# Attention values taken four blocks at a time beside the recurrence's outputs, and keys rounded once

## The chip, the cores and the metric

The kernel runs on one core of a Trainium2 chip. The metric is the device time of one execution in microseconds (us). The engines are TensorE (PE in the profile, its weight loads PEld), VectorE (DVE), ScalarE (ACT), GpSimd (POOL) and the DMA queues that SyncE (SP) feeds. Each engine takes its instructions in the order in which the kernel writes them, and waits at semaphores.

## The reference

One layer of a hybrid backbone on 256 context tokens (two tiles of 128) and 1024 latent tokens (eight tiles). After a joint input projection come two kinds of heads, then an output projection and a squared-ReLU MLP. The part in question is between the two projections:

```python
# gated linear attention, 8 heads, both directions, chunk by chunk
b = cumsum(g); A = tril(sum_d q*exp(b) * k*exp(-b))
o = (q*exp(b)) @ S + A @ v
S = exp(b_last)*S + (k*exp(b_last-b)).T @ v
# windowed attention, 8 query heads on 2 key heads, blocks of 128 queries
s = concat(q @ k_window.T (masked), q @ k_cache.T) * 64**-0.5
p = softmax(concat(s, sink))
o = p[:, :span] @ v_window + p[:, span:] @ v_cache
```

## The kernel before, in words

`mixer` (L1491) interleaves both. A **unit** u is one tile of 128 queries with one of the two key heads: 20 units, 16 of latent tiles with six or seven key blocks, then four of context tiles with two. That makes 116 blocks. A **slot** w (0 to 57, with two more to drain) takes two blocks. Every engine has its own loop over the slots, and the order inside a slot is written out by hand:

- PE, L1847 onwards. `scores` (L1796) makes the transposed scores of blocks 2w and 2w+1 in `st`: two full products each, a third for the mask. `values` (L1817) multiplies the probabilities of a block with the value rows: 16 small products on tiles of 128*64, accumulated in `pv`. Between them lie two **places**, `ahead((w, 0))` and `ahead((w, 1))`, with the work for later units: `raw_context` and `raw_local` (L1763, L1770), a pair of products whose row maxima are wanted; `queries` (L1755), four transposes; `turn_peaks` (L1781).
- The recurrence's step x (3 to 19) has its scores in slot 2(x-3) (`pe_scores`, L1258: four transposes of the decayed keys, then 16 products on tiles of 64*128) and its outputs in the slot behind (`pe_outputs`, L1276: 64 products on tiles of 128*64). Up to slot 33 an even slot is thus scores of the recurrence, an odd one its outputs.
- ACT: `weights` (L1895) is the exponential of one block's scores into `pT`, a ring of PRING = 4; `high_queries` (L1883) rounds turned queries; `outputs` (L1901) copies a finished unit's `pv`; `act_turned`, `act_output`, `act_decays` serve the recurrence.
- DVE: `top_context` and `top_local` (L1963, L1971) reduce the pair of products of a place to row maxima, `peaks`, `low_queries` and `spread` (L1992, L1958, L2008) prepare a unit, `finish` (L2015) divides. Behind both places of an even slot comes `dve_scores` (L1378: the causal mask on the recurrence's scores), behind those of an odd one `dve_new` (L1360: the state's update, one instruction for each half of the partitions).
- POOL has the recurrence's state and operands, and from slot 5 on, every third slot or so, the merging of finished outputs (`GlaOutput`, L1020); ACT waits in `GlaOutput.act` (L1067) for what SP loads for it.

The places use two banks, `score[:, 0]` and `score[:, 1]`; a product waits (`wait_room`) until the maxima of the last user of its bank are taken. A bank of `st` waits for the exponential before last. Ahead of slot 0 come six **beats** with steps 0 to 2 of the recurrence and seven groups of keys (`Keys`, L1409), which ACT copies twice: rounded into `kdup`, and rounded into the upper half of `khl`.

The PE order of a slot before:

## Time and profile before

| what | value |
|---|---|
| time, median of 3 runs | 1687.52 us (1684.58 to 1689.86) |
| the profiled execution's own time | 1684.21 us |
| its span | 1682.3 us |
| PE busy | 1603.9 us, 95% |
| PE weight loads busy | 1394.7 us, 83% |
| DVE, ACT, POOL busy | 1020.3, 673.6, 1016.3 us |
| beats | 390 to 415.2 us |
| slots 0 to 57 and the drain | 415.2 to 697.5 us |

A busy share says only that an instruction was under way; PE's matmuls overlap, so their durations don't add up, and the distance from one start to the next is what a group of them costs. Which wait binds is read in the order of time.

### The profile page before, as it was taken

Reading aid. Unit: us, or ns where it says so; the run is one execution under the profiler, and the core shown is the slowest. Engines: PE = TensorE matmul, PEld = TensorE weight load, DVE = VectorE, ACT = ScalarE, POOL = GpSimd, SP = SyncE. Lnnn points to the kernel's source line nnn. Section 1 sums busy time; section 2 is a strip of 40 time slices with the busy share of each in tenths; the row PEclk is TensorE's granted clock in tenths of the full one; section 3 lists DMA queues with packets and bytes.
Section 4 is the critical chain, followed back from the end, with each engine's and each line's share of the span. In section 5 each row is a group of like instructions: output and inputs, shape, how many; then the busy total and the mean of one; then the engine's idle time right before and its main releaser. Section 6 shows DMA issues by size and latency. Waiting matters only on the chain.

```text
span 1682.3 us, 31906 instructions
## 1 busy us (share of the span) xinstructions
PE 1603.9 (95%) x11618; PEld 1394.7 (83%) x11618; DVE 1020.3 (61%) x1584; ACT 673.6 (40%) x1192; POOL 1016.3 (60%) x758
## 2 busy tenths in 40 slices
PE   4999999998999888899999999999999999999997
PEld 1998778996777766788888998989978899998996
DVE  2713565666676669455866566575695545545468
ACT  2514224225444345312354444444535444444441
POOL 1711554654574789002487787777898667667682
PEclk9999999999999999999999999999999999999999
DMA  9254565659555455333661322313235132231322
GB/s 331 92 159 137 196 210 175 224 179 263 160 171 158 158 158 152 108 130 142 200 224 57 100 75 75 100 51 99 88 114 174 51 100 72 78 100 50 99 64 100
DMA packets 211450, 225.93 MB, mean 134 GB/s; under 512 B 52752, under 2 KB 171664, under 8 KB 208144
## 3 DMA queue, kind: packets, MB, share of 16 engines
q1 hardware_dynamic: 209248, 224.46, 41.6%
q8 instruction: 70, 1.15, 0.3%
q10 hardware_dynamic: 2096, 0.02, 0.1%
q14 instruction: 36, 0.29, 0.1%
HBM read 177.22 MB, written 47.24 MB: 133 GB/s over the span
## 4 chain that ended last, share of the span: by engine, by line
PE 43%; POOL 4%; DVE 2%; issue 1%; ACT 0%; DMA 0%; SPq 0%; DVEq 0%; ACTq 0%; POOLq 0%
PE ff_banks L3095 8%; PE ff_banks L3096 8%; PE ff_banks L3097 8%; PE ff_banks L3068 7%; PE ff_banks L3070 7%; PE ff_banks L3069 7%; POOL h_whi L2734 1%; POOL h_xop L2332 1%; POOL h_wlo L2746 1%; POOL h_whi L2741 1%; DVE ff_tmp L2935 1%; DVE ff_acc L2925 0%; DMA ff_hb<-in_w_ff 0%; DVE ff_acc L2919 0%; DVE ff_acc L2892 0%
## 5 line engine op out<-in xcount | busy, mean ns | idle before, releaser
L3068 PE MATMUL ff_banks<-h_xop,h_whi 128*128 128x320 f32 x888 | 275.2, 310 | 5.8 <-DVE wo_raw L2872 3.1
L3070 PE MATMUL ff_banks<-h_xop,h_whi 128*128 128x320 f32 x888 | 274.4, 309 | 0.0
L3069 PE MATMUL ff_banks<-h_xop,h_whi 128*128 128x320 f32 x888 | 274.4, 309 | 0.0
L2892 DVE TENSOR_TENSOR ff_acc<-ff_acc,ff_banks 128x512 f32<-128x512 f32 x294 | 199.0, 681 | 99.2 <-PE ff_banks L3097 99.2
L3095 PE MATMUL ff_banks<-h_wlo 128*128 128x512 f32 x600 | 234.3, 390 | 1.6 <-DVE ff_acc L2892 0.8
L3097 PE MATMUL ff_banks<-h_wlo 128*128 128x512 f32 x600 | 233.5, 389 | 0.0
L2734 POOL TENSOR_TENSOR h_whi<-mid_raw,h_whi 128x512 fp32r<-128x512 f32 x149 | 207.2, 1406 | 1.4 <-ACT h_whi L2586 1.4
L2746 POOL TENSOR_TENSOR h_wlo<-mid_raw,h_wlo 128x320 fp32r<-128x320 f32 x128 | 116.6, 913 | 129.6 <-ACT mid_raw L2623 129.6
L3068 PEld LDWEIGHTS ff_banks<-h_xop,h_whi 128*128 128x128 f32 x888 | 166.7, 188 | 9.5 <-issue 4.8
L3069 PEld LDWEIGHTS ff_banks<-h_xop,h_whi 128*128 128x128 f32 x888 | 166.7, 188 | 1.1
L3070 PEld LDWEIGHTS ff_banks<-h_xop,h_whi 128*128 128x128 f32 x888 | 166.7, 188 | 0.0
L972 PE MATMUL prj_banks<-prj_whi,h_hi 128*128 128x304 f32 x480 | 147.8, 308 | 3.3 <-DVE h_lo L341 2.2
L2734 POOL TENSOR_TENSOR h_whi<-ff_tmp,h_whi 128x512 fp32r<-128x512 f32 x63 | 105.5, 1674 | 67.7 <-ACT h_whi L2586 67.7
L974 PE MATMUL prj_banks<-prj_whi,h_lo 128*128 128x304 f32 x480 | 145.2, 303 | 0.0
L973 PE MATMUL prj_banks<-prj_wlo,h_hi 128*128 128x304 f32 x480 | 144.7, 301 | 0.0
L3095 PEld LDWEIGHTS ff_banks<-h_wlo 128*128 128x128 f32 x600 | 112.6, 188 | 25.8 <-DVE ff_acc L2892 1.9
L3096 PE MATMUL ff_banks<-h_whi,h_wlo 128*128 128x512 f32 x340 | 132.4, 389 | 0.0
L3097 PEld LDWEIGHTS ff_banks<-h_wlo 128*128 128x128 f32 x600 | 112.6, 188 | 23.6
L2586 ACT ACTIVATE h_whi<-mid_raw 128x512 fp32r<-128x512 f32 x149 | 89.9, 622 | 97.7 <-DVE mid_raw L2848 91.4
L2616 ACT ACTIVATE mid_raw<-wo_raw 128x320 f32<-128x320 f32 x128 | 60.3, 471 | 160.0 <-DVE wo_raw L2870 66.4
L3096 PE MATMUL ff_banks<-h_wlo 128*128 128x512 f32 x300 | 117.0, 390 | 0.0
L825 ACT ACTIVATE prj_stage<-prj_banks 128x304 f32<-128x304 f32 (+2 forms) x47 | 21.0, 446 | 220.7 <-PE prj_banks L974 133.9
(306 smaller groups left out, 3774.2 us busy)
## 6 DMA issues: line engine op xcount, KB each, us to landing
mid_raw<-in_w_ff SPq DMA_DIRECT2D x124, 512.0 KB, 4.3
mid_raw<-in_w_ada SPq DMA_DIRECT2D x18, 1024.0 KB, 7.2
early_room<-qk_by_channel SPq DMA_DIRECT2D x20, 512.0 KB, 4.1
proj<-prj_stage SPq DMA_DIRECT2D x60, 152.0 KB, 1.9
mid_raw<-in_w_in SPq DMA_DIRECT2D x6, 1216.0 KB, 7.2
early_room<-in_w_ada SPq DMA_DIRECT2D x6, 1024.0 KB, 10.9
decays<-early_room SPq DMA_DIRECT2D x8, 640.0 KB, 4.5
early_room<-decays SPq DMA_DIRECT2D x20, 256.0 KB, 2.9
```

The lines of the kernel that those rows point to most:

```text
L972: pe.matmul(out, x_hi, whi[j][:, k, 0:w], start=(k == 0), stop=False)
L973: pe.matmul(out, x_hi, wlo[j][:, k, 0:w], start=False, stop=False)
L974: mm = pe.matmul(out, x_lo, whi[j][:, k, 0:w], start=False, stop=(k == KD - 1))
L2734: pool.tensor_tensor(lo, source(q, i), hi.bitcast(F32), ALU.subtract).then_inc(w1lo_ready, 1)
L2746: pool.tensor_tensor(ulo[j][c][:, t0:t0 + TH], v[i % 2], uhi[j][c][:, t0:t0 + TH].bitcast(F32), ALU.subtract).then_inc(ulo_ready, 1)
L2892: dve.tensor_tensor(acc[:, p, at], acc[:, p, at], down[n % RING], ALU.add).then_inc(added, 1)
L3068: pe.matmul(out, w_hi[:, k], x_hi[:, k], start=(k == 0), stop=False)
L3069: pe.matmul(out, w_hi[:, k], x_lo[:, k], start=False, stop=False)
L3070: mm = pe.matmul(out, w_lo[:, k], x_hi[:, k], start=False, stop=(k == KH - 1))
L3095: pe.matmul(out, x_hi, w_hi[c][:, at], start=(c == 0), stop=False)
L3096: pe.matmul(out, x_hi, w_lo[c][:, at], start=False, stop=False)
L3097: mm = pe.matmul(out, x_lo, w_hi[c][:, at], start=False, stop=(c == 1))
```

## The change

1. PE's order in a slot becomes: place 0, scores of both blocks, the recurrence's four transposes (`pe_turned`, split off `pe_scores`), place 1, the recurrence's 16 score products, values, the recurrence's outputs, values of a second unit.
2. Values are taken in odd slots alone, four blocks at a time (2w-4 to 2w-1), up to slot 51; from slot 52 two in every slot again. PRING goes from 4 to 6.
3. ACT rounds queries of place 0 before the exponentials of its slot, and copies the turned keys of the recurrence before it rounds queries of place 1 and copies a unit's `pv`.
4. The state's update is put into 256 adjoining columns of its bank, so that one DVE instruction over 128 partitions takes it, where there were two over 64.
5. Keys are copied once by ACT, over all partitions of `khl`; DVE then writes the remainder over its lower half. `kdup` is gone.
6. The places are dealt out anew from the changed `done_slot` and `last_scores`: `finish` of a unit moves to the slot behind its last values, always even up to slot 52.

```diff
-    def pe_scores(self, pe, x):
+    def pe_turned(self, pe, x):
         i, d, t = self.place(x)
         pe.wait_ge(self.ke_ready, x + 1)
         if x:
-            pe.wait_ge(self.new_ready, 2 * x)
+            pe.wait_ge(self.new_ready, x)
         for b in range(self.HP):
             tr = pe.transpose(self.ps[:, 2, b * P:(b + 1) * P], self.ke[:, d, b], self.keep["ident"])
         tr.then_inc(self.tr_ready, 1)
+
+    def pe_scores(self, pe, x):
+        i, d, t = self.place(x)
         pe.wait_ge(self.qe_ready, x + 1)
...
-                mm = pe.matmul(self.ps[rows, 2, c:c + DH], self.kt[:, d, c:c + DH], self.v[:, j, c:c + DH], start=True, stop=True)
+                mm = pe.matmul(self.ps[rows, 2, b * DH:(b + 1) * DH], self.kt[:, d, c:c + DH], self.v[:, j, c:c + DH], start=True, stop=True)
...
-        for half in range(2):
-            rows = slice(half * DH, (half + 1) * DH)
-            upd = self.ps[rows, 2].rearrange("p (b c) -> p b c", c=P)[:, :, half * DH:(half + 1) * DH]
-            dve.tensor_tensor(self.new[rows], upd, self.decayed(d, t, rows, 2), ALU.mult).then_inc(self.new_ready, 1)
+        dve.tensor_tensor(self.new[:, :, :], self.update(), self.decayed(d, t, slice(0, P), 2), ALU.mult).then_inc(self.new_ready, 1)
...
     def act(self, act, n):
         act.wait_ge(self.tr_ready, n + 1)
-        act.activation(self.keys_of(self.kdup, slice(0, P), n), self.turned(slice(0, P), n), ACT.Copy).then_inc(self.dup_ready, 1)
-        act.activation(self.keys_of(self.khl, slice(0, DH), n), self.turned(slice(0, DH), n), ACT.Copy).then_inc(self.hl_ready, 1)
+        act.activation(self.keys_of(self.khl, slice(0, P), n), self.turned(slice(0, P), n), ACT.Copy).then_inc(self.hl_ready, 1)
...
-    QRING, PRING = 4, 4
+    QRING, PRING = 4, 6
...
+        SINGLE = begin[LONG] // 2 - 2
+
+        def group(w):
+
+            if not 1 <= w <= SLOTS or (w % 2 == 0 and w < SINGLE):
+                return []
+            return list(range(max(0, 2 * w - 4) if w % 2 and w <= SINGLE else 2 * w - 2, 2 * w))
...
-                while u + 1 >= QRING and at[0] < done_slot[u + 1 - QRING] - 1:
+                while u + 1 >= QRING and at[0] < last_scores[u + 1 - QRING]:
...
+        def parts(w):
+
+            first = [g for g in group(w) if unit_of[g] == unit_of[group(w)[0]]]
+            return first, group(w)[len(first):]
...
+                    ahead((w, 0))
                     if w < SLOTS:
                         scores(2 * w)
                         scores(2 * w + 1)
-                    ahead((w, 0))
-                    late = 1 <= w <= SLOTS and crossing(w)
-                    if 1 <= w <= SLOTS:
-                        values(2 * w - 2)
-                        if not late:
-                            values(2 * w - 1)
-                    if w == 0:
+                    if w in scores_at:
+                        rec.pe_turned(pe, scores_at[w])
+                    ahead((w, 1))
+                    now, late = parts(w)
+                    if w in scores_at:
                         rec.pe_scores(pe, scores_at[w])
-                    ahead((w, 1))
-                    if w and w in scores_at:
-                        rec.pe_scores(pe, scores_at[w])
+                    for g in now:
+                        values(g)
                     if w in outputs_at:
                         rec.pe_outputs(pe, outputs_at[w])
-                    if late:
-                        values(2 * w - 1)
+                    for g in late:
+                        values(g)
...
                 for w in range(SLOTS + 2):
+                    if (w, 0) in query_at:
+                        high_queries(query_at[w, 0])
                     if w < SLOTS:
                         weights(2 * w)
                         weights(2 * w + 1)
-                    if (w, 0) in query_at:
-                        high_queries(query_at[w, 0])
+                    if w in scores_at:
+                        rec.act_turned(act, scores_at[w])
+                    if (w, 1) in query_at:
+                        high_queries(query_at[w, 1])
                     for u in ending(w):
                         outputs(u)
                         sink_term(u)
-                    if (w, 1) in query_at:
-                        high_queries(query_at[w, 1])
-                    if w in scores_at:
-                        rec.act_turned(act, scores_at[w])
```

DVE's and POOL's order inside a slot is as before.

## Rows read from the trace of the kernel before

**Rows 1.** Windows of beats, slots 0-23, 24-33, 34-57 (columns in its header).
```profile
core 0: us, PE busy (x) PEld busy (x) DVE busy (x) ACT busy (x) POOL busy (x), PEclk, DMA share, GB/s
390.00:415.23 25.23, 19.68 (x266) 16.56 (x266) 21.68 (x43) 14.66 (x29) 16.27 (x18) 0.86 0.91 249
415.23:549.43 134.20, 128.88 (x1964) 102.00 (x1960) 91.83 (x194) 59.75 (x118) 79.87 (x84) 1.00 0.52 164
549.43:611.35 61.92, 55.93 (x833) 44.14 (x829) 40.12 (x83) 24.76 (x50) 51.56 (x50) 0.97 0.44 146
611.35:697.50 86.15, 73.62 (x994) 55.34 (x990) 64.23 (x122) 46.33 (x90) 57.44 (x46) 0.98 0.52 160
```

**Rows 2.** Timeline of PE, slots 14 to 16: start, duration (us), engine, line, operation.
```profile
494.65 0.50 PE L1810 MATMUL mix_st<-mix_qdup,mix_khl 128*128 128x512 f32 x1
...
495.76 1.15 PE L1828 MATMUL mix_pv<-mix_vx,mix_pT 128*64 128x65 f32 x32
496.85 0.73 PE L1768 MATMUL mix_score<-mix_khl,mix_qdup 128*128 128x512 f32 x2
497.41 0.60 PE L1264 MATMUL mix_gla<-keep_mats,early_ke 128*128 128x128 f32 x4
497.94 1.16 PE L1272 MATMUL mix_gla<-early_qe,early_ke 64*128 64x128 f32 x16
499.04 0.49 PE L1810 MATMUL mix_st<-mix_qdup,mix_khl 128*128 128x512 f32 x1
...
500.29 0.52 PE L1778 MATMUL mix_score<-mix_khl,mix_qdup 128*128 128x384 f32 x2
...
501.82 1.01 PE L1768 MATMUL mix_score<-mix_khl,mix_qdup 128*128 128x512 f32 x2
502.75 0.69 PE L1285 MATMUL mix_gla<-early_room,early_kt 128*64 128x64 f32 x16
...
505.18 0.49 PE L1810 MATMUL mix_st<-mix_qdup,mix_khl 128*128 128x512 f32 x1
```

**Rows 3.** Timelines of PE's weight loads, 32 and 16 values, and of scores between full tiles.
```profile
500.73 1.01 PEld L1828 LDWEIGHTS mix_pv<-mix_vx,mix_pT 128*64 128x64 f32 x32 [0.25 <-ACT mix_pT L1899]
512.49 0.55 PEld L1828 LDWEIGHTS mix_pv<-mix_vx,mix_pT 128*64 128x64 f32 x16 [0.36 <-ACT mix_pT L1899]
...
418.70 0.39 PE L1810 MATMUL mix_st<-mix_qdup,mix_khl 128*128 128x512 f32 x1
...
419.63 1.04 PE L1768 MATMUL mix_score<-mix_khl,mix_qdup 128*128 128x512 f32 x2
```

**Rows 4.** Timeline of DVE, slot 15.
```profile
499.22 1.23 DVE L1383 TENSOR_TENSOR early_at<-mix_gla,keep_mats 128x1024 f32<-128x1024 f32 x1 [0.48 <-PE mix_gla L1272]
500.87 0.62 DVE L1985 CUSTOM_DVE_ANT_0 mix_junk<-mix_score,mix_maskr,mix_topc 128x384 f32<-128x384 f32 x1 [0.42 <-PE mix_score L1778]
...
502.36 1.29 DVE L1969 TENSOR_REDUCE mix_topc<-mix_score 128x1 f32<-128x512 f32 x2
503.56 0.86 DVE L1367 TENSOR_TENSOR mix_new<-mix_gla,keep_dec 64x256 f32<-64x256 f32 x2
```

**Rows 5.** Timeline of PE, a place behind queries in slot 2; late values in slot 45.
```profile
429.31 0.47 PE L1768 MATMUL mix_score<-mix_khl,mix_qdup 128*128 128x512 f32 x1 [1.00 <-DVE mix_qlow L1960]
...
659.87 0.69 PE L1828 MATMUL mix_pv<-mix_vx,mix_pT 128*64 128x65 f32 x16 [1.17 <-ACT mix_sums L1905]
```

**Rows 6.** Timeline of ACT behind slot 24.
```profile
559.26 0.63 ACT L1071 ACTIVATE mid_raw<-mid_raw 128x512 f32<-128x512 f32 x1 [5.49 <-DMA mid_raw<-proj]
...
560.75 0.60 ACT L1887 ACTIVATE mix_qdup<-mix_score 128x512 fp32r<-128x512 f32 x1
```

**Rows 7.** Waits, 415 to 700: who waited for whom, total us, times, longest.
```profile
ACT mid_raw L1071 <- DMA mid_raw<-proj: 15.6, 4, 5.5
```

**Rows 8.** Timeline of DVE, beats.
```profile
397.72 0.88 DVE L1394 TENSOR_TENSOR mix_state_p<-mix_gla,keep_dec 64x256 f32<-64x256 f32 x2
...
407.17 0.88 DVE L1394 TENSOR_TENSOR mix_state_p<-mix_gla,keep_dec 64x256 f32<-64x256 f32 x2
```

More of the change, by code:

```diff
@@ L1316, in decayed, with update @@
         return self.dec[rows, d, :, t, which:which + 1].broadcast_to([rows.stop - rows.start, self.HP, DH])
+    def update(self):
+        return self.ps[:, 2, 0:self.HP * DH].rearrange("p (b c) -> p b c", c=DH)
     def dve_first(self, dve):
@@ L1334, in wait_state @@
         if x < 2:
-            eng.wait_ge(self.new_ready, 2 * x + 2)
+            eng.wait_ge(self.new_ready, x + 1)
         else:
@@ L1354, in pool_state @@
         pool.tensor_tensor(self.kept[:, :, :], st[:, d], self.decayed(d, t, slice(0, P), 1), ALU.mult).then_inc(self.kept_ready, 1)
-        pool.wait_ge(self.new_ready, 2 * x + 2)
+        pool.wait_ge(self.new_ready, x + 1)
         pool.wait_ge(self.kept_ready, x - 1)
@@ L1390, in dve_state @@
             dve.wait_ge(self.ds_ready, x + 1)
-            for half in range(2):
-                rows = slice(half * DH, (half + 1) * DH)
-                upd = self.ps[rows, 2].rearrange("p (b c) -> p b c", c=P)[:, :, half * DH:(half + 1) * DH]
-                dve.tensor_tensor(st[rows, d], upd, self.decayed(d, t, rows, 2), ALU.mult).then_inc(self.new_ready, 1)
+            dve.tensor_tensor(st[:, d], self.update(), self.decayed(d, t, slice(0, P), 2), ALU.mult).then_inc(self.new_ready, 1)
             return
@@ L1398, in dve_state @@
         dve.wait_ge(self.ds_ready, x + 1)
-        for half in range(2):
-            rows = slice(half * DH, (half + 1) * DH)
-            upd = self.ps[rows, 2].rearrange("p (b c) -> p b c", c=P)[:, :, half * DH:(half + 1) * DH]
-            dve.tensor_tensor(self.new[rows], upd, self.decayed(d, t, rows, 2), ALU.mult).then_inc(self.new_ready, 1)
-        dve.wait_ge(self.new_ready, 2 * x + 2)
+        dve.tensor_tensor(self.new[:, :, :], self.update(), self.decayed(d, t, slice(0, P), 2), ALU.mult).then_inc(self.new_ready, 1)
+        dve.wait_ge(self.new_ready, x + 1)
         dve.wait_ge(self.kept_ready, x - 1)
@@ L1423, in __init__, with work @@
         self.k_in, self.kc_in = s.sem("k_in"), s.sem("kc_in")
-    def work(self, s, keep, kdup, khl, kone, score, st, pv):
-        self.keep, self.kdup, self.khl, self.kone, self.score, self.st, self.pv = keep, kdup, khl, kone, score, st, pv
-        self.tr_ready, self.dup_ready, self.hl_ready, self.low_ready, self.one_ready = (s.sem("keys_" + n) for n in (
-            "tr_ready", "dup_ready", "hl_ready", "low_ready", "one_ready"))
+    def work(self, s, keep, khl, kone, score, st, pv):
+        self.keep, self.khl, self.kone, self.score, self.st, self.pv = keep, khl, kone, score, st, pv
+        self.tr_ready, self.hl_ready, self.low_ready, self.one_ready = (s.sem("keys_" + n) for n in (
+            "tr_ready", "hl_ready", "low_ready", "one_ready"))
     def room(self, n):
@@ L1514, in mixer @@
         rec.rest(s)
-        kdup = s.sb("kdup", [P, KV, NB * P], F32R)
         khl = s.sb("khl", [P, KV, NB * P], F32R)
@@ L1547, in mixer @@
         stored = ahead.mixed
-        keys.work(s, keep, kdup, khl, kone, score, st, pv)
+        keys.work(s, keep, khl, kone, score, st, pv)
         glo = GlaOutput(s, keep, a, scratch, *(arena[:, 2 * m * GW:2 * (m + 1) * GW].rearrange("p (j n) -> p j n", j=2) for m in range(4)),
@@ L1579, in mixer @@
         first_slot = [begin[u] // 2 for u in range(U)]
-        done_slot = [(begin[u] + count[u] - 1) // 2 + 1 for u in range(U)]
+        last_scores = [(begin[u] + count[u] - 1) // 2 for u in range(U)]
+        SINGLE = begin[LONG] // 2 - 2
[3 more added lines that the diff above has]
+            return list(range(max(0, 2 * w - 4) if w % 2 and w <= SINGLE else 2 * w - 2, 2 * w))
+        assert [g for w in range(SLOTS + 1) for g in group(w)] == list(range(total)), (SINGLE, [group(w) for w in range(SLOTS + 1)])
+        value_slot = {g: w for w in range(SLOTS + 1) for g in group(w)}
+        done_slot = [value_slot[begin[u] + count[u] - 1] for u in range(U)]
+        assert len(set(done_slot)) == U
         BEATS = 6
@@ L1836, in _ @@
                         if k % 2 == 0:
+                            rec.pe_turned(pe, k // 2)
                             rec.pe_scores(pe, k // 2)
```

12 lines of the change are left out of this document (5 added, 7 removed).

## The prediction, made before the changed kernel was run

> **What bounds the kernel now.** I read the page first: PE is busy 95% of the span, so whatever the change brings must come out of PE's order of time. The windows [rows 1] then show that the stretch that the change touches, beats and slots, lasts 307.5 us. PE is busy 129 of 134 us in slots 0 to 23, but DVE too is at 92, and in slots 24 to 33 POOL is at 52 of 62. No engine waits for nothing here; three are nearly full.
>
> The timeline of PE [rows 2] and that of DVE beside it [rows 4] show how they interlock. A place's pair of products keeps both banks of `score` until DVE has reduced them: 1.29 us for the cache's scores (at 502.36), 1.4 us for the window's (500.87 to 502.3), and 0.6 us pass from the product's start to the reduction's (500.29 to 500.87). The next place's first product waits for the first maximum, its second for the second. In the odd slot 15 DVE is late, because the mask on the recurrence's scores (1.23 us) comes first in its order: PE's 16 score products end at 499.04, the mask runs 499.22 to 500.45, the first place's maxima run to 502.3, and the second place, issued at 501.82, is held until 502.75. Before the change PE has the 1.09 us of `values` in that gap; what is left open is 0.93 us for a pair that costs 0.56 elsewhere (496.85 to 497.41).
>
> **The change, part by part.** I write R for the moment when the recurrence's score products end.
>
> *Switches between tile shapes.* Values between full tiles last 1.09 us [rows 2]. Their 16 further weight loads take 1.01 - 0.55 = 0.46 us [rows 3], so 32 products are worth 0.92, and 0.17 goes in leaving. The scores in front of them, with a change of shape on either side, last 1.11 us (494.65 to 495.76) [rows 2] against 0.93 between full tiles [rows 3]: 0.18 more. A trip to the small tiles and back costs 0.35 us. Every slot up to 33 makes one for its values; afterwards none does, since those of the odd slots adjoin the outputs. Slots 34 to 51 make nine in place of 18, and the late half of slot 38 had one. That is 33 + 9 + 1 = 43 trips, 15.1 us.
>
> The profile shows the 0.35 us as a late start. The Trainium skill, "TensorEngine Tiling (Array Packing)", section "Key Properties", says that changing the tiling mode drains TensorE; by that rule alone the change would gain all 43 trips, which is the first rival.
>
> *The common pair of slots (14 and 15 and their like).* Even slot, afterwards: scores 1.04 (one change of shape), transposes 0.53, place 0.56, score products 1.10 [rows 2]: 3.2 us; before it was 499.04 - 494.65 = 4.39. Odd slot, afterwards: the place 1 of the even slot is issued 1.66 before R, DVE has reduced it at R + 0.25, the mask ends at R + 1.5, the first place's maxima at R + 2.2 and R + 2.9, so the second place's second product starts at R + 2.95, and values at R + 3.3. PE by itself would be there at R + 2.2. Four blocks take 1.84, the outputs 505.18 - 502.75 = 2.43: R + 7.6. Before it was 6.14 (499.04 to 505.18). The pair takes 10.8 after 10.5. The 0.7 us of two trips is gone, and a wait of 1.1 has come in place of 0.4, because values no longer fill it. The values of an odd slot moved behind the second place; that is the step on which all hangs.
>
> *The other pairs, laid out in the same way.* Their times before are distances between starts of scores in the same timeline, of which [rows 2] show three; [rows 1] have their sum. Slots 8 and 9: 11.0 after 12.8, because before an exponential stood ahead of the rounded queries there. Slots 2 and 3: 12.6 and 12.6; PE had waited 1.00 [rows 5] for ACT's two exponentials, which now stand behind; the first place of slot 3 now pays the mask. Where queries and peaks come in place 1 of an even slot (10, 16, 22), ACT rounds them only after two exponentials and the copy of the turned keys, and DVE has remainder, spread (0.7 each) and mask in a row: maxima start at R + 2.7, values at R + 4.4: 12.4 to 12.6 after 11.5, 11.9 and 11.6. Where they come in place 1 of an odd slot (7, 13, 19), the peaks wait for the first place: values at R + 3.5, 11.2 to 11.35 after 10.2, 11.1 and 10.7. Slots 4 and 5: 11.2 and 11.2. Slots 20 and 21, all four places full: 11.1 after 10.1. Slots 0 and 1: 10.0 and 10.0. Slots 2 to 23 sum to +3.7 us.
>
> *Slots 24 to 33.* At slot 24 ACT waits for a load of the merging until 559.26 [rows 6], 9.8 us after the outputs end. Before, PE went on to slot 26 before it missed the rounded queries. Now they are in place 0 of slot 25, 3.6 us behind the outputs, and values and outputs stand behind the place that needs them: values at 12.7, the pair 17.0 after 11.0. Slots 26 and 27 give 2.2 back (10.7 after 12.9), 28 and 29 2.3 (12.7 after 15.0, which had a wait for POOL), 30 and 31 cost 0.2, 32 and 33 0.3. Sum: 63.9 after 61.9 [rows 1], +2.0. POOL's own work there, 51.6 us, would allow less but not much less than 60.
>
> *Slots 34 to 57.* Ten trips give 3.5 back. Queries rounded ahead of exponentials give about 0.5 in each of 34, 47 and 53, and the load of slot 36 is issued earlier, as no store stands before it: 1.2 over slots 34 to 37. Against it: a unit's last values and the next one's first adjoin in slots 35, 39, 45 and 49, with ACT's copy (0.39 and its way, 0.7 to 1.2) between, as at 659.87 [rows 5]: 3.6 for 1.2. Place 1 of an even slot and place 0 of the next now adjoin with no work between: about 1 us each in 35, 39, 41 and 43. My sum is 86.2 after 86.1 [rows 1]: +0.1.
>
> *Beats.* ACT saves seven copies of some 0.48, which it does at a stretch; the chain there runs over DVE, which saves 0.44 at 397.72 and again at 407.17 [rows 8], and 0.2 by the earlier rounding: slot 0 starts some 1.2 us earlier. The remainder is computed as before. In the slots the same merged update (0.86 for two [rows 4]) lies under the outputs, in which DVE has nothing else to do: nothing. If that cover failed it would be worth 0.44 a pair.
>
> *Sum.* -1.2 + 0 + 3.7 + 2.0 + 0.1 = +4.6 us. The profiled execution took 1684.2 us in all, 3.3 under the median of 1687.5, so it becomes 1688.8, and the median **1692.1 us**. What follows the slots is bound by PE and shifts with them.
>
> **Rivals.** *The trips count in full.* If the second place of an odd slot waits no longer than before, the gain is 15.1 + 1.2 less 2.4 for the late values: -13.9, 1673.6 us; with half of the new waits it would be about 1682. For it: DVE is only 68% busy, so that a reordering may find room. Against it: DVE's order is not changed, and the mask stands ahead of the maxima in every odd slot [rows 4].
>
> *They cancel.* PE's new waits take just what the switches gave, POOL sets the pace in 24 to 33, beats give 1: 1687 us. For it: POOL's 52 of 62 us.
>
> *ACT's waits for loads come out on PE (slower).* Slot 24's 5.5 us wait [rows 6] is one of four, 15.6 us in all [rows 7]. In every odd slot values and outputs now stand behind a place that may need ACT's rounding; before, the values stood ahead of it. If each of the other three costs 3 us as in slot 25, and the recurrence's state, started later, delays POOL by 2, the sum is +4.6 + 9 + 2: 1703 us. It decides when a load lands more than 4 us behind the outputs. For it: the next load is issued while the recurrence's are under way. Against: three of the four lay in slots with a free place.
>
> *The change doesn't do what it says* can be left at the merged update: the same 256 columns in twice the partitions must take 0.42, not 0.86; if not, the beats give nothing.
>
> **How the numbers follow.** Forecast 0.37, give or take 5 us, as each pair is laid out to 0.3 us; trips in full or half 0.26; cancel 0.17; loads 0.20. What a measurement of this kernel can tell from no change is about 0.3%, 5 us: 1682.5 to 1692.6. The forecast lies half inside it. Faster: the first rival and a little: 0.28. Same: cancel and half the forecast: 0.34. Slower: the rest, 0.38. The range of 8 in 10 goes from half way into the first rival to half way to the last: 1677 to 1700 us.
>
> **What would show it.** PE's timeline of slots 14 and 15: the second place of slot 15 must start its second product 2.9 us behind R, with a wait put down to DVE's maximum; values start at R + 3.3 and last 1.84. The waits of PE for DVE's maxima must grow by some 10 us over the slots. Scores between full tiles must last 0.93. Slot 25 must show a stall of 5 us for the rounded queries. If values start at R + 2.3, the chain over DVE was wrong and the first rival holds; if slots 24 to 33 take under 62 us, the step on loads was.

## The result, and the profile after

The changed kernel takes 1712.28 us in the median of four runs (1710.40 to 1719.08), the kernel before in the same comparison 1686.59 (1684.58 to 1689.86). The ratio is 1.0158, with a 95% interval of 1.0125 to 1.0190: slower by 26 us. The forecast had the sign and missed the size: +4.6, and a range that ended at 1700.

The page of the changed kernel, first lines (busy time of each engine, its share of the span, and instructions):

```profile
span 1710.9 us, 31877 instructions
## 1 busy us (share of the span) xinstructions
PE 1612.0 (94%) x11618; PEld 1400.2 (82%) x11618; DVE 1010.1 (59%) x1564; ACT 670.4 (39%) x1185; POOL 1014.2 (59%) x758
```

The span grew by 28.6 us, PE's busy time by only 8: the time is in PE's waits. DVE has 10 us less to do; the merged update accounts for most of that. To see where the time went, I cut both traces at the same places, the first score product of slots 2, 24, 34 and 57. Windows of the kernel before, then of the changed one: slots 2 to 23, then 34 to 56; the changed kernel has slots 24 to 33 between (columns as in [rows 1]).

```profile
425.24:549.43 124.19, 119.34 (x1832) 94.45 (x1828) 83.78 (x173) 55.57 (x110) 73.17 (x74) 1.00 0.51 161
...
611.35:693.21 81.86, 69.33 (x918) 51.78 (x914) 63.47 (x119) 43.41 (x83) 57.44 (x46) 0.98 0.54 165
```

```profile
427.78:557.57 129.79, 117.56 (x1829) 94.14 (x1826) 80.67 (x163) 55.12 (x111) 73.89 (x74) 0.99 0.49 154
...
557.57:625.14 67.57, 56.55 (x834) 45.10 (x832) 38.84 (x78) 24.84 (x51) 51.78 (x50) 0.92 0.41 134
625.14:722.72 97.58, 76.00 (x912) 55.08 (x910) 59.40 (x118) 42.90 (x83) 53.60 (x45) 0.91 0.45 139
```

| stretch | before | after | difference | forecast |
|---|---|---|---|---|
| ahead of the beats | 389.99 | 391.56 | +1.6 | 0 |
| beats, up to slot 0's scores | 25.24 | 26.57 | +1.3 | -1.2 |
| slots 0, 1 | 10.01 | 9.65 | -0.4 | 0 |
| slots 2 to 23 | 124.19 | 129.79 | +5.6 | +3.7 |
| slots 24 to 33 | 61.92 | 67.57 | +5.7 | +2.0 |
| slots 34 to 56 | 81.86 | 97.58 | +15.7 | +0.1 |
| behind that | | | -0.9 | 0 |

The tail, slots 34 to 56, holds more than half, and there the forecast had nothing. In slots 2 to 23 PE is busy 1.8 us less and idle 7.4 more (12.2 for 4.85). In the tail it is idle 9.1 more and busy 6.7 more, at a granted clock of 0.91 instead of 0.98.

PE's timeline of slot 15 in the changed kernel shows the step on which the forecast said all hung (its answer in the kernel before is [rows 2]); the first row is place 0, issued as the recurrence's 16 score products end:

```profile
503.63 0.65 PE L1786 MATMUL mix_score<-mix_khl,mix_qdup 128*128 128x384 f32 x2
504.11 0.40 PE L1818 MATMUL mix_st<-mix_qdup,mix_khl 128*128 128x512 f32 x1
...
505.72 0.47 PE L1776 MATMUL mix_score<-mix_khl,mix_qdup 128*128 128x512 f32 x1 [0.28 <-DVE mix_topl L1992]
506.40 0.50 PE L1776 MATMUL mix_score<-mix_khl,mix_qdup 128*128 128x512 f32 x1 [0.21 <-DVE mix_topl L1992]
506.82 2.09 PE L1836 MATMUL mix_pv<-mix_vx,mix_pT 128*64 128x65 f32 x64
508.74 0.64 PE L1288 MATMUL mix_gla<-early_room,early_kt 128*64 128x64 f32 x16
```

With R = 503.63 the second product starts at R + 2.8, the values at R + 3.2, and 64 of them take 1.92. The forecast had 2.95, 3.3 and 1.84. The marks in brackets add to only 0.5 us, because a wait is shown in full only where nothing of the engine's is still draining; the distances between starts give it: 505.72 to 506.82 is 1.10 for a pair that costs 0.56 elsewhere [rows 2], and it starts some 0.4 us later than behind scores without a wait.

In slots 24 and 25 the stall that the forecast named is there. The products of place 1 in slot 25 wait for rounded queries; the rows are PE's, then ACT's:

```profile
567.72 0.76 PE L1776 MATMUL mix_score<-mix_khl,mix_qdup 128*128 128x512 f32 x1 [5.17 <-DVE mix_qlow L1967]
```

```profile
565.74 0.63 ACT L1071 ACTIVATE mid_raw<-mid_raw 128x512 f32<-128x512 f32 x1 [5.54 <-DMA mid_raw<-proj]
566.28 0.58 ACT L1894 ACTIVATE mix_qdup<-mix_score 128x512 fp32r<-128x512 f32 x1
```

What it did not name is in the tail. Slot 37 first, ACT and then PE. PE's scores of that slot start at 638.39. ACT stands idle until they are through, and only then rounds the queries which place 1 needs (its pair starts at 640.90):

```profile
639.44 0.60 ACT L1894 ACTIVATE mix_qdup<-mix_score 128x512 fp32r<-128x512 f32 x1 [2.40 <-PE mix_st L1821]
```

```profile
638.39 0.48 PE L1818 MATMUL mix_st<-mix_qdup,mix_khl 128*128 128x512 f32 x1
...
640.90 0.47 PE L1776 MATMUL mix_score<-mix_khl,mix_qdup 128*128 128x512 f32 x1 [1.10 <-DVE mix_qlow L1967]
```

The rounded queries go into a ring of four units, `qdup`, so the rounding waits until the unit four before has made its last scores. The planner (the code that deals the places out) puts queries at the earliest into the slot of those scores. Before the change the scores stood ahead of place 0, so they were made by then; now they stand behind it. This happens four times in the tail, in slots 37, 44, 47 and 53; in the list of waits further down `ACT mix_qdup <- PE mix_st` is its row (three times by L1821, 6.4 us, and once by L1819, 2.4).

Slots 41 to 43 hold the longest wait of PE in the tail; it is that of place 0 of slot 43, at 668.20. First PE's rows, then ACT's, then DVE's:

```profile
658.14 1.09 PE L1786 MATMUL mix_score<-mix_khl,mix_qdup 128*128 128x256 f32 x2 [1.22 <-DVE mix_topc L1976]
659.16 3.38 PE L1836 MATMUL mix_pv<-mix_vx,mix_pT 128*64 128x65 f32 x64
...
668.20 0.36 PE L1786 MATMUL mix_score<-mix_khl,mix_qdup 128*128 128x256 f32 x1 [4.06 <-DVE mix_topc L1976]
```

```profile
662.59 0.39 ACT L1912 ACTIVATE mix_sums<-mix_pv 128x260 f32<-128x260 f32 x1 [5.02 <-PE mix_pv L1836]
...
662.97 1.05 ACT L1132 ACTIVATE h_whi<-wo_raw 128x1024 fp32r<-128x1024 f32 x1
```

```profile
664.05 1.23 DVE L1140 TENSOR_TENSOR h_wlo<-wo_raw,h_whi 128x1024 fp32r<-128x1024 f32 x1 [4.18 <-ACT h_whi L1132]
...
667.38 1.27 DVE L1976 TENSOR_REDUCE mix_topc<-mix_score 128x1 f32<-128x512 f32 x2
```

Read it from the top. Place 1 of slot 41 waits 1.22 us for maxima and holds the values back. The values, 64 of them at a mean granted clock of 0.57, take 3.3 us, and ACT stands 5.02 us for them to copy the unit's sums. Behind that copy is queued the rounding of an output weight; for that DVE stands 4.18; behind DVE's part of the weight stand the unit's division and the maxima of slot 42; and PE waits 4.06 for those. Weight, division and maxima stand in this order on DVE before the change too; what moved on PE is that the values come four blocks at a time and behind place 1.

Waits in both tails, from the view of waits (who waited for whom, total us, times, longest). Kernel before:

```profile
ACT mix_sums L1905 <- PE mix_pv L1828: 4.2, 7, 0.8
PE mix_score L1778 <- DVE mix_qlow L1960: 3.6, 4, 1.7
```

Changed kernel:

```profile
ACT mix_sums L1912 <- PE mix_pv L1836: 12.5, 6, 5.0
ACT mix_qdup L1894 <- PE mix_st L1821: 6.4, 3, 3.3
PE mix_score L1786 <- DVE mix_topc L1976: 6.0, 5, 4.1
PE mix_score L1786 <- DVE mix_qlow L1967: 5.6, 4, 1.6
```

### The profile page after: what moved, and what is told of

Read it like the earlier page. It is cut to its first block and busy times, and to the rows that moved or that the text cites. A ratio compares the mean times of both kernels' runs of the same rounds, so it can differ in the third digit from the quotient of the medians.

```text
span 1710.9 us, 31877 instructions
## 1 busy us (share of the span) xinstructions
PE 1612.0 (94%) x11618; PEld 1400.2 (82%) x11618; DVE 1010.1 (59%) x1564; ACT 670.4 (39%) x1185; POOL 1014.2 (59%) x758
```

## The experiments

The tail below is counted from the first scores of slot 34 to those of slot 57: 81.86 us before, 97.58 changed. Some expectations count it 0.5 us sooner and 2.2 later, which is 100.3 for the changed kernel. Each batch ran beside the kernel before on the same chip; its medians there were 1686.5, 1689.4, 1689.3 and 1687.2 us. Every edit is made to the changed kernel unless it says otherwise.

### The tail: groups, clock, weights

**Values two blocks at a time from slot 34.**

```diff
-        SINGLE = begin[LONG] // 2 - 2
+        SINGLE = 2 * X - 6
```

> Kernel after with one edit: from slot 34 on, values of two blocks in every slot, as before the change; all else as after. In the trace of after, slots 34 to 57 took 100.3 us for 84.1 before. Theory A, grouping and ACT's order: four blocks of values stand behind a held place, ACT's copy of a finished unit waits for them (34.9 us in all, for 8.2 before), and the exponentials, the output weights and so DVE's and PE's next place stand behind that copy. It expects most of the 16 us back: slots 34 to 57 at 84 to 88 us, the kernel at 1697 to 1701. Theory B, the new dealing of places and PE's new order with the two places of neighbouring slots adjoining, which this edit leaves: it expects 96 us and more there, the kernel above 1708. Theory C, a mere fall of TensorE's clock: the time comes back only as far as the idle stretches go.

1710.26 us (1707.62 to 1712.74), ratio 1.0150 (1.0133 to 1.0167). Its tail:

```profile
623.64:717.46 93.82, 75.46 (x912) 54.18 (x909) 60.78 (x118) 42.81 (x83) 54.62 (x45) 0.89 0.46 144
```

In the profiled run the tail is 3.8 us shorter. That much isn't shown to be the groups of four: the profiled run was the fastest of the four, the median fell by only 2.0, and the two ratios' intervals overlap. Some 12 of the tail's 15.7 us have another cause.

**Two idle products of 512 columns ahead of place 1 in slots 34 to 56**, to keep PE at work where it waits:

```diff
+                    if X * 2 - 6 <= w < SLOTS - 1:
+                        if w == X * 2 - 6:
+                            pe.wait_ge(rec.at_ready, X)
+                        for _ in range(2):
+                            pe.matmul(rec.ps[:, 1], khl[:, 0, 0:P], khl[:, 1, 0:HALF], start=True, stop=True)
                     ahead((w, 1))
```

> Kernel after, with two idle products of 512 columns ahead of place 1 in each slot from 34 to 56; nobody reads what they write. By themselves they cost 0.46 us a slot, 10.6 us over 23 slots, where PE is not waiting. Theory C, the clock: TensorE ran at a mean of 0.91 of its clock in slots 34 to 57 of after, for 0.98 before; if the lower clock is the cause, the filled kernel gets it back and is no slower than after, perhaps 3 us faster. Theory A: PE waits anyway, so the products are half hidden, and the time goes up by 0 to 6 us, with the clock at 0.97 or more.

1716.12 us (1712.46 to 1718.11), ratio 1.0181 (1.0160 to 1.0201). Its tail:

```profile
624.99:724.24 99.25, 81.02 (x959) 59.72 (x956) 57.98 (x118) 43.00 (x83) 54.04 (x45) 0.97 0.44 136
```

The granted clock is 0.97 again instead of 0.91, and the tail is 1.7 us longer, not shorter. PE's longest wait for `topc`, 4.2 us, is still there. So the lower clock isn't what makes the waits.

**Two of the output weights' roundings one slot later** (41 to 42, 45 to 46), which takes the weight out of the chain shown for slots 41 and 42:

```diff
-        wo_at = dict(zip((37, 38, 40, 41, 44, 45, 48, 50), range(D // P)))
+        wo_at = dict(zip((37, 38, 40, 42, 44, 46, 48, 50), range(D // P)))
```

> Kernel after, with the splitting of output weights moved from slots 41 and 45, in which a unit ends, to 42 and 46. In the trace of after DVE waits 4.2 us at slot 41 for ACT's part of it, which stands behind the copy of the finished unit, and PE then waits 4.1 us for a maximum. Theory A expects this wait to go: 3 to 8 us less than after, 1704 to 1709. If the output weights are not the link, the time stays at 1712 within 2.

1711.00 us, but from 1706.11 to 1715.87 in four runs, ratio 1.0157 (1.0126 to 1.0188). In the profiled run (1707.17) the wait of 4.06 is 1.55:

```profile
666.37 0.35 PE L1786 MATMUL mix_score<-mix_khl,mix_qdup 128*128 128x256 f32 x1 [1.55 <-DVE mix_topc L1976]
```

and the tail takes 90.8 us. So the link from the weight to this wait is as read. The profiled execution is 5.5 us shorter than that of the changed kernel, but it differs in slots that the edit doesn't touch as well (28 and 29: 16.3 us for 14.0), and that the median gains is not shown.

### The tail: PE's order

**The old order of a slot from slot 34 on**, with two-block values:

```diff
-                    ahead((w, 0))
+                    old = w >= 2 * X - 6
+                    if not old:
+                        ahead((w, 0))
                     if w < SLOTS:
                         scores(2 * w)
                         scores(2 * w + 1)
+                    if old:
+                        ahead((w, 0))
...
+                    now, late = parts(w)
+                    if old:
+                        for g in now:
+                            values(g)
+                        now = []
                     ahead((w, 1))
-                    now, late = parts(w)
```

> The changed kernel with, from slot 34 on, TensorE's old order of a slot (scores, place 0, values, place 1) and values of two blocks; the slots before, the six buffers, the keys, the updates and ScalarE's order stay as changed. Theory A (TensorE's new order of the tail is what costs: a place stands right behind the scores there and waits for the queries' rounding and for the evictions of the place before): the tail takes 84 to 88 us after 100.3, the kernel 1695 to 1700. Theory B (ScalarE's new order, the six buffers or the lower clock cost, TensorE's order doesn't): the tail stays over 95 us and the kernel over 1707.

1696.85 us (1694.87 to 1699.77), ratio 1.0048 (1.0034 to 1.0061): 15.4 us of the 26 are gone. The tail is below the range given (83.7 by that count):

```profile
626.21:707.18 80.97, 70.62 (x919) 52.91 (x915) 63.17 (x118) 42.85 (x83) 56.34 (x45) 0.96 0.54 167
```

**Only the values ahead of place 1 in the tail** (two blocks; place 0 stays ahead of the scores). This version lies between that with two-block values and that with the old order:

```diff
+                    now, late = parts(w)
+                    if w >= 2 * X - 6:
+                        for g in now:
+                            values(g)
+                        now = []
                     ahead((w, 1))
-                    now, late = parts(w)
```

> The changed kernel with values of two blocks from slot 34 on, and there the values ahead of place 1; place 0 stays ahead of the scores. It differs from the version with place 1 right behind the scores (two-block values, tail 96.5) in one move, and from the old order (tail 84) in the other. Theory A (place 1 right behind the scores is what costs, since nothing covers the evictions of place 0): tail 84 to 89, kernel 1696 to 1702. Theory B (place 0 ahead of the scores costs: it holds the scores back while it waits for DVE, and the queries' rounding then waits for scores behind it): tail 93 to 97, kernel 1706 to 1711. In halves: about 90 and 1703.

1702.17 us (1697.86 to 1703.62), ratio 1.0076 (1.0048 to 1.0103).

```profile
626.55:712.32 85.77, 73.28 (x912) 51.15 (x910) 63.79 (x118) 42.77 (x83) 56.05 (x45) 0.96 0.51 158
```

Its waits in the tail:

```profile
ACT mix_qdup L1898 <- PE mix_st L1821: 13.2, 4, 6.1
```

The tail's steps are therefore 97.58 (changed), 93.82 (two-block values), 85.77 (values ahead of place 1), 80.97 (scores ahead of place 0): 3.8, 8.0 and 4.8 us, taken away in this order. The medians (1712.3, 1710.3, 1702.2, 1696.9) give 2.0, 8.1 and 5.3. How far one trace can be trusted shows in the kernel further down whose tail is the changed kernel's, instruction for instruction: it took 100.34 us there for 97.58. So the groups of four are not told from noise; both moves of PE's order cost, and place 1 right behind the scores costs more. With scores ahead of place 0 the row `ACT qdup <- st` is gone; ACT waits there for the turned queries themselves.

**Queries not before place 1 of the slot of the old unit's last scores:**

```diff
-                while u + 1 >= QRING and at[0] < last_scores[u + 1 - QRING]:
+                while u + 1 >= QRING and at < (last_scores[u + 1 - QRING], 1):
```

> The changed kernel; the planner may no longer put queries of a unit into place 0 of the slot in which the unit four before it makes its last scores, so where their rounding had to wait for scores of the same slot (slots 37, 44, 47, 53) they go to place 1. Theory A1 (that wait, 1.1 to 1.6 us at four slots, is part of the tail's loss): the tail is 4 to 7 us shorter than 100.3, the kernel 1705 to 1709. Theory A2 (the wait moves to the next place, or evictions bound the tail anyhow): less than 2 us of change, the kernel 1710 to 1714.

1707.14 us (1707.01 to 1708.41), ratio 1.0109 (1.0080 to 1.0138); tail 92.62:

```profile
625.65:718.27 92.62, 74.81 (x912) 55.13 (x909) 59.52 (x118) 42.77 (x83) 54.08 (x45) 0.91 0.47 146
```

The wait for a place in the ring of queries is worth about 5 us (5.0 in the tail, 5.1 in the median), by one comparison in the plan.

### Slots 0 to 33: values beside the outputs, or ahead of place 1

**In odd slots up to 33 the four-block values ahead of place 1**, so that they are between scores and a full product again and cost one trip more:

```diff
+                    now, late = parts(w)
+                    if w % 2 and w in outputs_at:
+                        for g in now:
+                            values(g)
+                        now = []
                     ahead((w, 1))
-                    now, late = parts(w)
```

> The changed kernel with the four-block values of the odd slots up to 33 ahead of place 1 instead of behind it, so one trip more in each of 16 odd slots, and the values give the evictions of place 0 their time. By the forecast's own terms: a trip costs 0.35 us, place 1 then waits 0 to 0.3 instead of 0.21 to 1.1, the probabilities are asked for 1.2 us sooner; sum -8 to +4 us, and -3 is taken: 1707 to 1711. Rival (the place's wait was already small, all that comes is the trip): +6 us, 1716 to 1719. Rival (values now wait for the exponentials): 1 us in each odd slot, over 1720.

1698.81 us (1696.71 to 1704.84), ratio 1.0064 (1.0041 to 1.0087): 13.5 us less, where 3 were expected. Slots 2 to 23, and slot 15's values and second place:

```profile
426.89:547.24 120.35, 115.03 (x1828) 92.86 (x1826) 81.08 (x163) 54.90 (x111) 73.83 (x74) 1.00 0.53 166
```

```profile
497.89 2.09 PE L1836 MATMUL mix_pv<-mix_vx,mix_pT 128*64 128x65 f32 x64
499.90 0.74 PE L1776 MATMUL mix_score<-mix_khl,mix_qdup 128*128 128x512 f32 x2
500.57 0.69 PE L1288 MATMUL mix_gla<-early_room,early_kt 128*64 128x64 f32 x16
```

Slots 2 to 23 take 9.4 us less than in the changed kernel, and 3.8 less than before the change. While PE makes the values, to 499.90, DVE ends the mask and the first place's maxima, at 498.9, and place 1 then starts without a wait. PE's waits at the places of slots 2 to 23 sum to 11.7 us in the changed kernel and 5.0 here. The expectation had taken the waits as smaller than they are; slots 6 and 7 alone, where DVE is held up, give 2.5 us (11.8 for 14.3).

**The old order on PE everywhere; of the new order on PE only the groups of four in odd slots up to 33 stay** (so do ACT's new order, the six buffers, the new plan of the places and parts 4 and 5):

```diff
-                    ahead((w, 0))
                     if w < SLOTS:
                         scores(2 * w)
                         scores(2 * w + 1)
+                    ahead((w, 0))
+                    now, late = parts(w)
+                    for g in now:
+                        values(g)
+                    now = []
                     if w in scores_at:
                         rec.pe_turned(pe, scores_at[w])
                     ahead((w, 1))
-                    now, late = parts(w)
```

(and two-block values from slot 34.)

> The changed kernel with the old order on TensorE everywhere (scores, place 0, values, place 1; the keys' transposes of the recurrence beside its scores) and two-block values from slot 34; what is left of the new order is that values come four blocks at a time in every second slot up to 33. It differs from the version with both repairs (1680.7) in place 0 and the transposes alone. Theory A (the gain over the kernel before is that of the fewer trips for values, some 11 trips of 0.35 us and the waits that go): slots 2 to 23 in 120 to 123, the kernel 1681 to 1686. Rival (place 0 ahead of the scores and the transposes between the places bring half of it): slots 2 to 23 in 124 to 128, the kernel 1686 to 1691.

1679.34 us (1677.91 to 1683.11), ratio 0.9956 (0.9941 to 0.9970): faster than the kernel before.

```profile
429.33:549.44 120.11, 114.86 (x1833) 93.13 (x1829) 80.04 (x162) 54.69 (x110) 73.68 (x74) 1.00 0.53 166
```

4.1 us less than before in eleven pairs of slots, a mean of 0.37 a pair. That mean is not the price of a trip. The pairs range from 2.6 us less (slots 8 and 9) to 2.0 more (6 and 7), and ACT's earlier rounding alone, in the last experiment below, takes 1.6 of the 4.1. The price can be read in slots 14 and 15, where little else changed. PE's timeline there:

```profile
496.26 0.50 PE L1818 MATMUL mix_st<-mix_qdup,mix_khl 128*128 128x512 f32 x1
...
499.39 0.50 PE L1818 MATMUL mix_st<-mix_qdup,mix_khl 128*128 128x512 f32 x1
...
501.11 2.09 PE L1836 MATMUL mix_pv<-mix_vx,mix_pT 128*64 128x65 f32 x64
503.12 0.73 PE L1776 MATMUL mix_score<-mix_khl,mix_qdup 128*128 128x512 f32 x2
503.79 0.39 PE L1288 MATMUL mix_gla<-early_room,early_kt 128*64 128x64 f32 x6
```

Against [rows 2] the even slot is 1.26 us shorter (3.13 for 4.39) and the values of the odd slot 0.93 longer (2.01 for 1.08): 0.33 for the trip. Another 0.26 comes from place 1, which no longer waits (0.67 for 0.93).

Place 0 ahead of the scores and transposes between the places bring nothing here (120.11 against 120.35 with them).

**Both repairs**, values ahead of place 1 up to 33 and the old order from 34 on:

> The changed kernel with both repairs: in the odd slots up to 33 the values ahead of place 1, from slot 34 on the old order and two-block values. If the two add up (-13.5 and -15.4 against the changed kernel's 1712.3): 1682 to 1686, slots 2 to 23 in 120.4, slots 24 to 33 in 64.7, the tail in 84 to 85; below the kernel before by 0 to 4. Rival (they overlap, or the second gain was the clock's): 1687 to 1692.

1680.70 us (1677.08 to 1685.55), ratio 0.9960 (0.9938 to 0.9982). Slots 0 to 33 take 192.2 us, the tail 80.9. The two gains add up; neither was the other's clock.

### Slots 24 to 33: ScalarE's waits for loads

All of these have both repairs, but the last. The merging in slot 24 is moved to 25; then those of 8, 24, 27, 30 each by one; then the tail's too:

```diff
-        glo_at = dict(zip((5, 8, 24, 27, 30, 33, 36, 39, 42, 46), range(NT)))
+        glo_at = dict(zip((5, 8, 25, 27, 30, 33, 36, 39, 42, 46), range(NT)))
...
+        glo_at = dict(zip((5, 9, 25, 28, 31, 33, 36, 39, 42, 46), range(NT)))
...
+        glo_at = dict(zip((5, 9, 25, 28, 31, 34, 37, 40, 43, 46), range(NT)))
```

> As the version with both repairs, and the third merging of the recurrence's outputs in slot 25 instead of 24. Theory A (in slots 24 and 25 TensorE stands 4.3 us for queries whose rounding is queued on ScalarE behind its wait for the merging's load, and one slot later that wait stands behind the rounding): slots 24 and 25 take 12 to 13.5 us after 17.1, the kernel 1678 to 1682. Rival (the load's wait then holds the exponentials of slot 26, and the time comes back there): less than 1.5 us of gain, 1682 to 1686.

> As the version with both repairs, and the mergings of slots 8, 24, 27 and 30 each one slot later (9, 25, 28, 31). Theory A (each of these waits for loads on ScalarE comes out on TensorE, since rounding of queries or exponentials is queued behind it): 1676 to 1681, with the 1.8 us wait for rounded queries in slot 28 gone. Rival (only slot 24's is worth moving; the others move their wait into the next slot): 1679 to 1684, as with slot 24's alone.

> As the version with both repairs and four mergings one slot later, with the tail's mergings moved too (34, 37, 40, 43 for 33, 36, 39, 42). In the version with four moved, slots 24 to 33 took 55.3 us, but ScalarE then stood 8.5 us for the load of the merging in slot 36 and slots 36 and 37 took 13.4 instead of 8.4. Theory A (a merging whose load is asked for only one slot ahead of it is what stops ScalarE, so that each needs its two slots): slots 36 and 37 are back at 8.5 to 9.5, slots 24 to 33 stay at 55 to 56, the kernel 1673 to 1677. Rival (the loads are late wherever the merging stands in the tail, whose slots are short): the 5 us turn up in another slot of the tail, the kernel 1677 to 1681.

| mergings at | median us | ratio to before | slots 24, 25 | 28, 29 | 24 to 33 | tail |
|---|---|---|---|---|---|---|
| 8, 24, 27, 30 | 1680.70 | 0.9960 (0.9938 to 0.9982) | 17.09 | 14.17 | 62.95 | 80.89 |
| 8, 25, 27, 30 | 1678.13 | 0.9942 (0.9927 to 0.9958) | 10.86 | 18.38 | 60.96 | 81.00 |
| 9, 25, 28, 31 | 1678.84 | 0.9948 (0.9934 to 0.9962) | 10.88 | 12.33 | 55.34 | 86.07 |
| the tail's too | 1677.81 | 0.9948 (0.9931 to 0.9965) | 10.85 | 12.34 | 55.36 | 84.66 |

Slots 24 and 25 lose the whole stall, 6.2 us, and 4.2 come back in 28 and 29. With four mergings moved, slots 24 to 33 take 55.3 us, below the 60 that the forecast thought POOL would set, but 5.2 return in the tail. ACT's waits for the merging's loads: the sum in the second of these kernels, the longest one in the timeline of the third (14.0 us in all), the sum and one of slot 43 in the fourth:

```profile
ACT mid_raw L1071 <- DMA mid_raw<-proj: 12.6, 3, 6.3
```

```profile
620.01 0.63 ACT L1071 ACTIVATE mid_raw<-mid_raw 128x512 f32<-128x512 f32 x1 [8.48 <-DMA mid_raw<-proj]
```

```profile
ACT mid_raw L1071 <- DMA mid_raw<-proj: 13.7, 4, 5.6
```

```profile
645.77 0.63 ACT L1071 ACTIVATE mid_raw<-mid_raw 128x512 f32<-128x512 f32 x1 [4.88 <-DMA mid_raw<-proj]
```

The sum is 17.7 us with no merging moved, then 12.6, 14.0 and 13.7: the first move takes 5 us of it, the others move it to other slots. The four medians lie within 3 us and their intervals overlap, so no gain over both repairs is shown. In the last kernel slots 36 and 37 are back at 7.75, and slots 44 to 47 take 21.2 us instead of 16.2. The rival of the last of these expectations holds: the loads are late wherever the tail's mergings stand. A cure would have to issue them sooner, or take ACT's part of the merging out of the queue ahead of the rounding; that was not tried.

**The kernel before, with its merging of slot 24 in 25:**

> The kernel before with the third merging in slot 25 instead of 24. In it the queries due in slot 25 are ready long before, so ScalarE's 5.5 us for the load cost TensorE only 0.3 us in slot 26. Theory A: no gain (1685 to 1690, ratio 0.998 to 1.002), perhaps the loads' order changed as in the repaired version, where 4.2 us came back in slots 28 and 29: then up to 1692. Rival (the wait hurts the kernel before as much): 1682 to 1684.

1690.46 us (1685.01 to 1693.90), ratio 1.0023 (1.0006 to 1.0040). Slots 24 and 25 stay at 10.9, 28 and 29 go from 14.95 to 17.68, where PE waits 4.66 us for `topc`, and 30 and 31 from 12.64 to 14.70. In the kernel before ACT's wait in slot 24 is harmless, and the move itself brings the harm.

What makes that wait harmful is, as far as the runs tell, the new plan of the places, and not PE's order. The version above with the old order on PE has the stall too, and takes 16.80 us in slots 24 and 25; of the changed kernel's 6.7 us over the kernel before (17.73 for 11.00) only 0.9 go with the order. ACT's new order alone doesn't do it either (11.5 us, in the last experiment). The plan puts the queries into place 0 of slot 25 and their user into place 1; before, these were place 1 of 25 and place 0 of 26. PE's wait in the version with the old order, then in the kernel before:

```profile
559.99 0.52 PE L1776 MATMUL mix_score<-mix_khl,mix_qdup 128*128 128x512 f32 x1 [3.67 <-DVE mix_qlow L1970]
```

```profile
562.21 0.47 PE L1768 MATMUL mix_score<-mix_khl,mix_qdup 128*128 128x512 f32 x1 [0.34 <-DVE mix_qlow L1960]
```

In spite of the stall slots 24 to 33 take 59.87 us there, 2.1 less than before and 7.7 less than in the changed kernel. PE's new order therefore costs 7.7 us in this stretch, 5.9 of them in slots 26 to 33.

### The parts without PE's order

**The kernel before with the merged update and the keys rounded once** (parts 4 and 5 of the change alone):

> Kernel before with parts 4 and 5 of the change alone: the state's update as one DVE instruction and keys copied once. The prediction had -1.2 us for the beats and nothing in the slots. In the trace of after the beats lost 1.1 us to a lower clock and so showed nothing of it. Expected: 1685.4, that is 0 to 2 us under before. Rival: the halved updates, 17 of them with 0.44 us each, come out in full: 7 us.

1687.98 us in ten runs (1685.05 to 1690.30), ratio 1.0006 (0.9993 to 1.0019); the beats take 24.96 us for 25.24. These two parts are worth nothing that can be told.

**The same, and ACT rounds place 0's queries ahead of the exponentials:**

```diff
                 for w in range(SLOTS + 2):
+                    if (w, 0) in query_at:
+                        high_queries(query_at[w, 0])
                     if w < SLOTS:
                         weights(2 * w)
                         weights(2 * w + 1)
-                    if (w, 0) in query_at:
-                        high_queries(query_at[w, 0])
```

> The kernel before with the merged updates and the keys rounded once, and on ScalarE the rounding of place 0's queries ahead of the slot's exponentials instead of behind them; TensorE's order, the groups of values and the four buffers stay. Theory A (waits of TensorE for rounded queries behind exponentials are real cost in the kernel before: some nine slots with 0.5 to 1.0 us each): 1680 to 1684. Theory B (the exponentials then come 0.7 us later and the values wait as long): 1686 to 1692. If queries wait for the old unit's last scores, the exponentials queued behind them make it worse: over 1692.

1685.58 us (1682.82 to 1690.02), ratio 0.9982 (0.9966 to 0.9998). That lies between the ranges of the two theories. Slots 0 to 23 save 1.6 us by the profile (132.6 for 134.2), slots 24 to 33 lose 3.5 (65.4), where ACT's longest wait for a load is 6.0 us and PE's for `topc` 3.7. Whether the small gain is real is open.

## Why the prediction was right or wrong

**The price of a trip between shapes was right.** 0.35 us stood in the forecast, and 0.33 is what slots 14 and 15 save by it when their two groups of values are one and PE's order is the old one. The Trainium skill, "TensorEngine Tiling (Array Packing)", section "Key Properties", has a change of tiling mode drain TensorE; the trace agrees, at 0.33 us for a trip. The full 43 trips as a gain, the first rival, did not come.

**The step on which all hung was right in slots 2 to 23.** Slot 14 took 3.12 us for 3.2, slot 15 7.48 for 7.6 (503.63 to the end of the outputs at 511.11). PE's waits for DVE's maxima over all slots grew from 6.2 to 15.5 us, where some 10 more were forecast. That the values, moved behind place 1, no longer cover DVE's mask and maxima was the loss foreseen; putting them ahead again gave 9.4 us. This stretch exceeds the forecast by 1.9 us. Slots 6 and 7 are 3.0 over it (14.3 for 11.35), and the others together 1.1 under. In slot 7 DVE's sum of squares for the merging waits for POOL, and the maxima behind it in DVE's queue keep PE 2.46 us:

```profile
458.01 0.69 DVE L1090 TENSOR_REDUCE mix_glo_ssq<-mid_raw 128x8 f32<-128x512 f32 x1 [1.22 <-POOL mid_raw L1080]
```

```profile
459.38 0.63 PE L1768 MATMUL mix_score<-keep_mats,mix_xq 128*128 128x128 f32 x4 [2.46 <-DVE mix_topl L1992]
```

The forecast's account of DVE's queue names none of the merging's instructions.

**Slots 24 to 33: the stall was right, the stretch mis-sized**, +5.7 for +2.0. Slots 24 and 25 took 17.7 us for 17.0, with half the outputs at the lower clock behind the stall. The forecast gave two reasons for it: the queries' new place, which the runs support, and the values and outputs behind that place, which are worth 0.9 us. The other 3 us are slots 28 to 31 (27.8 for 25.5) and the pair behind: the queries of slots 28 and 31 are waited for 1.8 us each. With the old order on PE these slots 28 to 33 take 33.2 us for 39.1, so this too is PE's order.

**Slots 34 to 56: here the forecast failed**, at the step "my sum is 86.2 after 86.1". It knew from the common pair that a place right behind the scores is not covered, and charged that in the tail only where places adjoin with no work between, 1 us each in four slots. But in the tail every place 1 has just two blocks of scores ahead of it. Putting the values back ahead of it gave 8.0 us, twice the 4 that were charged. It saw that queries would be rounded ahead of exponentials and wrote down a gain of 0.5 us in 34, 47 and 53; it did not ask what else the rounding waits for. The scores that free the ring had been put behind the place that needs them: 5 us where the plan alone is repaired, a wait that the sum had at nothing. Putting place 0 back behind the scores gave 4.8; how much of that is the ring is not split. The forecast counted what waits for the scores on ACT, exponentials, and not the ring. The groups of four were taken as a gain of 3.5 us in trips less 2.4 for late values; undoing them made the kernel no slower. The chain over slots 41 to 43 shows one way in which they can cost: a unit's sums come later, and ACT's and DVE's queues stand behind those.

**The rival of loads** (1703) came in slot 25 only; of its other three slots none cost 3 us on PE. Its sum was nearest to the result, and not for its reason.

**Beats**: DVE's update took 0.42 us for 0.88 as foreseen (at 400.38 and 409.33). The 1.2 us did not come: +1.3 in the profiled run, where the granted clock of the beats was 0.81 for 0.86, and -0.3 with the two parts alone. Why so little came of it was not looked into.

## What to carry to other kernels

Work that one engine does between two dependent steps of another is cover; before moving it to save a switch, lay out what stands in the gap afterwards, and do this for every stage, not for the common pair alone. The saved trips were to be had without the move: with the values grouped where they stood, and all else that isn't PE's order as changed, the kernel was 0.4% faster than before. How much of that is the grouping and how much ACT's earlier rounding and the new plan is not split. The fastest versions, both repairs and mergings moved, took 1677.8 to 1678.8 us, 0.5 to 0.6% less than before and 2% less than the changed kernel. When the order of two steps is swapped, list for each ring and each bank who frees it, since a plan that counts in slots doesn't see an order inside a slot.

## What the runs showed of the hardware

The lower granted clock went with PE's own idle time: in the tail it was 0.98 before the change, with PE idle for 12.5 us, and 0.91 after it, with 21.6. 64 values took 1.92 us at 506.82, where PE's last waits had been 0.28 and 0.21 us and the granted clock was 1.00. They took 3.32 at 659.16, behind waits of 1.44 and 1.22 us, at a mean of 0.57; of the two levels, 2.4 and 1.2 GHz, that is mostly the lower. Two idle products a slot brought the tail's mean from 0.91 back to 0.97 and made it no shorter. ACT's waits for the mergings' loads came to 12.6 to 17.7 us in the four kernels with both repairs, and to 15.6 in the kernel before; moving one merging there by a slot brought them to 9.0 and made the kernel no faster.
